# A two-layer encoder trunk on one core: the first two weight units on a second DMA queue, the first tokens turned into two banks, a unit ahead of the parameters

## The reference

```python
def _hybrid_layer(x, cos, sin, ...):
    h = _rms_norm(x, norm_mix)
    z = jnp.einsum('bsd,de->bse', h, w_in)
    za, bq, bk, bv, cq, clat, ciq, cik, ciw, zd, zg = _split(z, IN_SIZES)
    ya = _gmlp_mixer(jax.nn.gelu(za), ...)
    yb = _swa_sink_mixer(bq, bk, bv, ..., cos, sin)
    yc = _dsa_mixer(cq, clat, ciq, cik, ciw, ..., cos, sin)
    yd = _pool_mixer(zd, d_w_group, d_scale)
    gates = jax.nn.sigmoid(zg).reshape(Bsz, S, N_BRANCH, D_MODEL)
    merged = gates[:, :, 0] * (ya @ a_w_out) + ... + gates[:, :, 3] * (yd @ d_w_out)
    x = x + merged @ w_o
    h2 = _rms_norm(x, norm_ffn)
    gate, up = jnp.split(h2 @ w_gate_up, 2, axis=-1)
    return x + (jax.nn.silu(gate) * up) @ w_down
```

## Time and profile before

| | us |
|---|---|
| median of 3 runs (lowest, highest) | 814.96 (814.76, 815.02) |
| the profiled run's own time | 815.25 |
| its span | 813.5 |
| PE busy | 805.1 (99%) |
| PE weight loads busy | 658.0 (81%) |
| DVE busy | 559.7 (69%) |
| ACT busy | 406.1 (50%) |
| POOL busy | 56.6 (7%) |

### The profile page before, as it was taken

One profiled execution on the slowest core, in us unless ns is written; L12 is line 12 of the kernel. 1 busy time (PEld: TensorE's weight loads), 2 busy tenths in 40 slices (PEclk: granted clock), 3 DMA queues, 4 the chain that ended last, 5 costly groups with the idle time before them and its releaser, 6 DMA issues.

```text
span 813.5 us, 10282 instructions
## 1 busy us (share of the span) xinstructions
PE 805.1 (99%) x3872; PEld 658.0 (81%) x3872; DVE 559.7 (69%) x854; ACT 406.1 (50%) x568; POOL 56.6 (7%) x103
## 2 busy tenths in 40 slices
PE   8999999999999999999999999999999999999998
PEld 6788777778888888888888887787788888888886
DVE  7799789877576554566568887898675754565443
ACT  5966655454274434444366644755543643444431
POOL 5850000000000000000005100000000000000000
PEclk9999999999999999999999999999999999999999
DMA  8654536545466555666663625474446555666541
GB/s 301 215 162 136 183 120 208 206 140 183 130 221 206 178 185 161 207 202 192 164 230 116 232 79 182 133 254 156 155 156 207 179 183 166 210 193 198 165 155 52
DMA packets 98976, 144.38 MB, mean 177 GB/s; under 512 B 11112, under 2 KB 62064, under 8 KB 98928
## 3 DMA queue, kind: packets, MB, share of 16 engines
q1 hardware_dynamic: 98928, 143.73, 54.6%
HBM read 142.54 MB, written 1.05 MB: 177 GB/s over the span
## 4 chain that ended last, share of the span: by engine, by line
PE 94%; DMA 2%; DVE 1%; ACT 1%; issue 1%; SPq 1%; ACTq 0%; DVEq 0%
PE big L1537 19%; PE big L1541 19%; PE big L1540 19%; PE mix L1541 10%; PE mix L1537 10%; PE mix L1540 10%; DMA w_raw<-in_w_in 1%; PE mix L1913 1%; PE mix L1581 1%; PE mix L1672 1%; DMA w_raw<-in_w_gate_up 1%; PE mix L1605 1%; PE mix L1593 1%; PE mix L1625 1%; PE mix L1658 1%
## 5 line engine op out<-in xcount | busy, mean ns | idle before, releaser
L738 ACT ACTIVATE w_hi<-w_raw 128x2048 fp32r<-128x2048 f32 (+2 forms) x140 | 255.0, 1827 | 155.4 <-DMA w_raw<-in_w_gate_up 89.6
L1049 DVE TENSOR_TENSOR w_lo<-w_raw,w_hi 128x2048 fp32r<-128x2048 f32 (+3 forms) x142 | 304.6, 2160 | 29.2 <-ACT w_hi L738 27.9
L1537 PE MATMUL big<-w_hi,act_hi 128*128 128x512 f32 (+2 forms) x476 | 185.7, 390 | 2.1 <-DVE w_lo L1049 2.1
L1541 PE MATMUL big<-w_hi,act_lo 128*128 128x512 f32 (+2 forms) x476 | 181.6, 381 | 0.0
L1540 PE MATMUL big<-w_lo,act_hi 128*128 128x512 f32 (+2 forms) x476 | 181.5, 381 | 0.0
L1537 PE MATMUL mix<-w_hi,act_hi 128*128 128x512 f32 x352 | 137.4, 390 | 0.0
L1541 PE MATMUL mix<-w_hi,act_lo 128*128 128x512 f32 x352 | 137.1, 390 | 0.0
L1540 PE MATMUL mix<-w_lo,act_hi 128*128 128x512 f32 x352 | 137.0, 389 | 0.0
L1537 PEld LDWEIGHTS big<-w_hi,act_hi 128*128 128x128 f32 x476 | 89.5, 188 | 22.6 <-DVE w_lo L1049 3.7
L1323 DVE TENSOR_TENSOR y_h_lo<-mix,y_h_hi 128x256 fp32r<-128x256 f32 x44 | 16.6, 420 | 127.7 <-ACT y_h_hi L968 127.7
L1541 PEld LDWEIGHTS big<-w_hi,act_lo 128*128 128x128 f32 x476 | 89.4, 188 | 17.2
(11 more groups left out here) (210 smaller groups left out, 718.6 us busy)
## 6 DMA issues: line engine op xcount, KB each, us to landing
w_raw<-in_w_in SPq DMA_DIRECT2D x44, 1024.0 KB, 5.1
w_raw<-in_w_gate_up SPq DMA_DIRECT2D x88, 512.0 KB, 4.8
w_raw<-in_w_down SPq DMA_DIRECT2D x22, 1024.0 KB, 4.9
w_raw<-in_w_o SPq DMA_DIRECT2D x8, 1024.0 KB, 4.9
w_raw<-in_b_w_out SPq DMA_DIRECT2D x4, 1024.0 KB, 6.3
w_raw<-in_w_in SPq DMA_DIRECT2D x4, 512.0 KB, 4.1
w_raw<-in_a_w_out SPq DMA_DIRECT2D x4, 512.0 KB, 3.5
w_raw<-in_d_w_out SPq DMA_DIRECT2D x4, 512.0 KB, 3.4
```

What stands on the lines that cost most here:

```text
L738: nc.scalar.activation(high(u)[:, a:b], arrived(u)[:, a:b], ACT.Copy).then_inc(hi_ready, 1)
L1049: nc.vector.tensor_tensor(low(u)[:, a:b], arrived(u)[:, a:b], high(u)[:, a:b].bitcast(F32), ALU.subtract).then_inc(lo_ready, 1)
L1537: ins = nc.tensor.matmul(dst[:, 0:w], xh, wh, start=first and n == 0, stop=False)
L1541: ins = nc.tensor.matmul(dst[:, 0:w], xl, wh, start=False, stop=end)
```

## The change

- The loads of units 0 and 1, four halves, are issued by ACT at the head of its program (`load_first`). On SP the tokens, the gain and the positions follow each other, then units 2, 3 and 4.
- Of the first four turned pieces, the last two go to another PSUM bank (`turned_at`). ACT starts once two are turned (`first_turned`). A copy of one element stands ahead, and the scaling of block 1 ahead of the copy of unit 0's second half; DVE and PE are ordered to match. The first projection's second half is taken in portions, both blocks after each.
- Unit 5 (the sixth) is issued ahead of the parameters. Seven parameters follow it; eight others follow unit 7, with a semaphore of their own, on which PE waits at slot 9 and DVE at slot 11.
- ACT squares block 0's tokens ahead of slot 0 and block 1's in slot 0, DVE takes the mean in slot 0, POOL's first power stands ahead of the last steps of the angles. The tables move to slot 2, behind that slot's steps and copies, and the change back to the exponential's table to slot 6.
- In layer 0 DVE ropes the indexer's heads at slots 3 and 4 instead of 2 and 3. At slot 4 the latent's norm now stands ahead of the rope, and the wait for the parameters with it, in both layers.

```diff
-N_PARAMS = 15
+N_PARAMS = 7
+N_LATE_PARAMS = 8
...
+        def turned_at(l, stage, tb, h, j):
+
+            if (l, stage, tb, h) == (0, "hT", 0, 0) and j >= 2:
+                return big[:, main_bank("proj", PROJ[0][0], 1), (j - 2) * P:(j - 1) * P]
+            return mix[:, mix_bank(stage, tb, h), j * P:(j + 1) * P]
...
-                if l == 0 and u < HALVED:
-                    for half, k in ((0, slice(0, 2)), (1, slice(2, 4))):
-                        sp.dma_start(dst[:, k, 0:b], w_in[l, rows, a:a + b].rearrange("(k p) n -> p k n", p=P)[:, k]
-                                     ).then_inc(first_in[u] if half == 0 else landed[s].sem, 16)
-                        if (u, half) == (0, 0):
-                            load_tokens(1, 0)
-                        elif (u, half) == (0, 1):
-                            for tb in range(TB):
-                                load_tokens(tb, 1)
-                            load_positions()
-                elif kind == "in":
+                if kind == "in":
...
-                    (g_ffn[:], norm_ffn[l].rearrange("(k p) -> p k", p=P)),
                     (g_lat[:], c_latent_gain[l].partition_broadcast(P)),
                     (g_head[:, 0], b_q_gain[l].partition_broadcast(P)),
                     (g_head[:, 1], b_k_gain[l].partition_broadcast(P)),
                     (g_head[:, 2], c_q_gain[l].partition_broadcast(P)),
                     (g_head[:, 3], c_k_gain[l].partition_broadcast(P)),
-                    (w_sp[:], a_w_spatial[l].rearrange("g i j -> i g j")),
...
+                assert len(params) == N_PARAMS
+                for dst, src in params:
+                    sp.dma_start(dst, src, allow_slow_non_contiguous=True).then_inc(params_in.sem, 16)
+
+            def load_late_params(l):
+                params = (
+                    (w_sp[:], a_w_spatial[l].rearrange("g i j -> i g j")),
...
+                    (g_ffn[:], norm_ffn[l].rearrange("(k p) -> p k", p=P)),
                 )
-                assert len(params) == N_PARAMS
+                assert len(params) == N_LATE_PARAMS
                 for dst, src in params:
-
-                    sp.dma_start(dst, src, allow_slow_non_contiguous=True).then_inc(params_in.sem, 16)
+                    sp.dma_start(dst, src, allow_slow_non_contiguous=True).then_inc(late_params_in.sem, 16)
...
             load_gain(0)
+            load_tokens(1, 0)
+            for tb in range(TB):
+                load_tokens(tb, 1)
+            load_positions()
             for l in range(DEPTH):
-                load_unit(l, 0)
-                load_unit(l, 1)
+
                 if l > 0:
+                    load_unit(l, 0)
+                    load_unit(l, 1)
                     load_params(l)
+                    load_late_params(l)
                 for u in range(2, NU):
                     load_unit(l, u)
-                    if (l, u) == (0, RING - 1):
+                    if (l, u) == (0, RING):
                         load_params(0)
+                    if (l, u) == (0, RING + 2):
+                        load_late_params(0)
...
                 at = flat[1]
+            power(0, "mix")
             for k, turn in enumerate(TURNS):
...
                 for name in NORMS:
-                    power(l, name)
                     if (l, name) == (0, "mix"):
                         averages_of_pools()
+                    else:
+                        power(l, name)
...
-                nc.scalar.activation(act_spare[:], minus_half[:, 0:1], ACT.Exp).then_inc(alone_act, 1)
+
+            def load_first(u):
+                _, a, b, h = UNITS[u]
+                rows = slice(h * PIECES * P, (h + 1) * PIECES * P)
+                for half, k in ((0, slice(0, 2)), (1, slice(2, 4))):
+                    act.dma_start(w_raw[:, u, k, 0:b], w_in[0, rows, a:a + b].rearrange("(k p) n -> p k n", p=P)[:, k]
+                                  ).then_inc(first_in[u] if half == 0 else landed[u].sem, 16)
...
-                bank = mix_bank("hT", tb, h)
-                act.wait_ge(*mix_is_full(0, "hT", tb, h))
                 for j in range(4):
                     k = 4 * h + j
-                    e = nc.scalar.activation(act_hi[:, k, tok(tb)], mix[:, bank, j * P:(j + 1) * P], ACT.Copy,
+                    if (tb, h, j) == (0, 0, 0):
+                        act.wait_ge(first_turned, 1)
+                    elif j == (2 if (tb, h) == (0, 0) else 0):
+                        act.wait_ge(*mix_is_full(0, "hT", tb, h))
+                    e = nc.scalar.activation(act_hi[:, k, tok(tb)], turned_at(0, "hT", tb, h, j), ACT.Copy,
                                              scale=g_mix[:, k:k + 1])
...
+                    for u in range(HALVED):
+                        load_first(u)
+
+                    act.wait_ge(warm_in, 1)
+                    nc.scalar.activation(act_spare[:], rope_t[:, 0, 0:1], ACT.Copy).then_inc(alone_act, 1)
                     act.wait_ge(gain_placed, 1)
                     first_gained(0, 0)
+                    first_gained(1, 0)
                     split(0, 0, 1)
-                    first_gained(1, 0)
                     first_gained(0, 1)
                     first_gained(1, 1)
                     split(0, 1, 1)
+                    x_squares(0, "mix", 0)
                 for s in range(SLOTS):
-                    if s in STEPS_FIRST:
+                    if s in STEPS_FIRST or (l, s) == (0, 2):
                         steps(l, s)
                     if s == WO + 4:
                         high_gained(l, "h2T", 1)
                     for ahead in splits_in(l, s):
                         split(*ahead)
-                    if (l, s) == (0, 1):
-                        for tb in range(TB):
-                            x_squares(0, "mix", tb)
+                    if (l, s) == (0, 0):
+                        x_squares(0, "mix", 1)
+                    if (l, s) == (0, 2):
                         tables()
-                    if s not in STEPS_FIRST:
+                    if s not in STEPS_FIRST and (l, s) != (0, 2):
                         steps(l, s)
+                    if (l, s) == (0, 6):
+
+                        act.wait_ge(alone_act, 1)
+                        nc.scalar.activation(act_spare[:], minus_half[:, 0:1], ACT.Exp).then_inc(alone_act, 1)
...
                 if s == 1:
                     scales(l, "mix", 0)
-                for tb in range(TB):
-                    if s == 2 + tb:
-                        if l == 0:
-                            dve.wait_ge(const_sin, 4)
-                        dve.wait_ge(*main_is_drained(l, "proj", "idx", tb))
-                        rope(l, "I", heads_a, roped_a, tb, 5, [(0, 4, 1, 0), (4, 5, 2, 4)], tb == 1)
                 if s == 3:
                     mean_of_sums(l, "lat", P)
+                if s == 4:
                     dve.wait_ge(*params_in.nth(l, params_in.per_layer))
-                if s == 4:
                     r = norm_factor(l, "lat")
                     for tb in range(TB):
                         ins = nc.vector.scalar_tensor_tensor(out=lat[:, tb, :], in0=lat[:, tb, :], scalar=r[:, tb:tb + 1],
                                                              in1=g_lat[:], op0=ALU.mult, op1=ALU.mult)
                     ins.then_inc(lat_normed.sem, 1)
+                for tb in range(TB):
+
+                    if s == 2 + tb + (1 if l == 0 else 0):
+                        if l == 0:
+                            dve.wait_ge(const_sin, 4)
+                        dve.wait_ge(*main_is_drained(l, "proj", "idx", tb))
+                        rope(l, "I", heads_a, roped_a, tb, 5, [(0, 4, 1, 0), (4, 5, 2, 4)], tb == 1)
...
+                    dve.wait_ge(*late_params_in.nth(l, late_params_in.per_layer))
...
                     split_high(0)
                     split(0, 0, 0)
                     first_low(0, 0)
+                    first_low(1, 0)
                     split(0, 0, 1)
-                    first_low(1, 0)
                     split_high(1)
                     split(0, 1, 0)
...
-                    if (l, s) == (0, 1):
+                    if (l, s) == (0, 0):
                         mean_of_sums(0, "mix", D_MODEL)
...
-                        ins = nc.tensor.transpose(mix[:, bank, j * P:(j + 1) * P], src[:, tb, k * P:(k + 1) * P],
+                        ins = nc.tensor.transpose(turned_at(l, stage, tb, h, j), src[:, tb, k * P:(k + 1) * P],
                                                   ident[:])
+                        if (l, stage, tb, h, j) == (0, "hT", 0, 0, 1):
+                            ins.then_inc(first_turned, 1)
...
-                    pe.wait_ge(*params_in.nth(l, params_in.per_layer))
+                    pe.wait_ge(*late_params_in.nth(l, late_params_in.per_layer))
...
                     turn(l, "hT", 0, [0])
                     products_of_zeros(2)
-                    first_products(0, 0)
                     turn(l, "hT", 1, [0])
```

(24 more changed lines are left out.)

9 lines of the change are left out of this document (2 added, 7 removed).

## The result

The changed kernel takes 816.09 us (median of 19 runs, 815.28 to 816.67) against 814.59 for the kernel before (19 runs, 813.88 to 815.3) on the same chip: ratio 1.0016, 95% interval 1.0010 to 1.0022. Its profiled execution took 815.43, span 813.7; that of before 815.25, span 813.5.

What follows compares the result with a forecast made beforehand. TensorE is busy 769.40 of 769.71 us from 36.29, so only the first 36.3 us can win. Terms -2.1, +0.2, +1.2, +0.7 sum to 0.0: 815.25 profiled, 815.0 median; 8-in-10 range 812.8 to 816.4.

Steps and rivals of the forecast that it cites:

- the sum: Whole kernel: -2.1 us at the start, +0.2 at unit 3, +1.2 at slot 5, +0.7 at unit 11, together 0.0.
- the slower rival: Positions no sooner, unit 0's subtraction ahead of them, unit 5's in the averages: R 40.2, +1.6 us, 816.6; chance 0.12.
- The chain that was to eat the lead: GpSimd's late latent power delays VectorE's rope to R, cutting TensorE's lead to 0.7 at slot 5 and 0.0 at unit 11.
- the wait at slot 5: Sign of being right: TensorE waits 1 to 3 us before the slot-5 transposes, released by VectorE's rope.
- The start: First 36.3 us: second projection at 19.5 instead of 21.57, a lead of 2.1 us, bounds 1.2 and 2.5.
- The positions: Fewer bytes deep on their queue, so GpSimd may take them 0.8 us sooner than 10.79; bounds 0 and -1.5.
- Unit 5: Issued at 15 instead of 25.99, it lands near 22 to 23, so TensorE's stall of 0.94 us goes.
- The block on GpSimd: Unit 5's subtraction on VectorE falls amid GpSimd's averages and prolongs a select: +2.06 us; latent's power at 35.7 to 36.8.
- R: Time when VectorE has done the latent and block 1's rope at slot 4: 38.2 to 39.3, taken as 38.6.
- The limit at unit 11: VectorE's full row up to unit 11's subtraction caps TensorE's lead at 38.6 - R, 0.0 us.
- The lead kept: Unit 5's subtraction comes after averages and power: R 36.5 to 37.0, lead 1.6 to 2.1, 812.9 to 813.4; chance 0.20.
- The engines' rate as the bound: DMA engines' rate bounds the start, tokens and weights come as before: lead 1.2, R about 39.1, 815.5 us; chance 0.13.

Runs made afterwards that it cites:

- one-queue run: The changed kernel with units 0 and 1 loaded on SyncE again, between the tokens as before: 815.18 us, 0.9997 times the kernel before.
- unit 5 sooner: The kernel before with one line changed, unit 5 issued ahead of the 15 parameters: 814.52 us, 0.9992 times the kernel before.
- power early: The changed kernel with GpSimd doing the mixer norm's power ahead of the third part of the angles' reduction: 816.04 us, 1.0012 times before.
- The fastest kernel: The changed kernel with one queue, rope ahead of latent's norm, last eight selects late and mixer norm's power early: 812.06 us, 0.9964 times before.
- the run that began later (20.59): The changed kernel with units 0 and 1 on SyncE's queue and block 1's rope ahead of the latent's norm in layer 0: 813.47 us, 0.9982 times before.

## Why the prediction was right, point by point

The time lies inside 812.8 to 816.4 and the difference inside what was called no change. But the interval, 1.0010 to 1.0022, does not reach 1: the changed kernel is 1.5 us slower, where the sum gave 0.0, and 816.09 is 1.1 above the forecast of 815.0 and 0.5 below the 816.6 of the slower rival. The chain that was to eat the lead is the one that did. Three of its terms were mis-sized and one step was read wrongly, and that the number held is in part luck, as said below.

Of the signs named beforehand these came: no table load right before the first scaling, the rope that waited for the latent's power, the select of 2.34 over unit 5's subtraction, and the short wait at unit 11. The first scaling (6.30 for 5.7) and the second projection (20.55 for 19.5) missed, the wait at slot 5 was 0.28 for 1 to 3, and the sign set down for the slower rival, a wait for unit 5, was there.

- **The start: 1.0 and not 2.1.** The steps within the engines nearly held: with one queue the second projection was at 19.81 at best, for 19.5 forecast. The main mis-sized term is the arrival of the gain (1.04 of waiting) and of block 1's tokens (0.85); most of it goes with the second queue, and the bound of 1.2 for just this case was still too kind. Over the traces the second projection is at 20.52 to 21.34 with two queues (six traces, mean 20.96, leaving out the one with the positions moved) and 19.81 to 20.59 with one (four, mean 20.18): the second queue costs 0.8 in the mean, as much as the start varies with either, where it was to give speed, and 0.7 of the shortfall against 19.5 is there without it. The engines do move more with it (251 GB/s from 2 to 4 us, where the earlier trace rows has 197), but the bytes that TensorE waits for come later.
- **The positions: 1.0 later and not 0.8 sooner** (11.77 against 10.79 in the earlier trace rows). Outside its bounds of 0 and 1.5 sooner. The rule of the Trainium skill that was weighed ("DMA: Bandwidth & Descriptors", "Issuing engines are not separate DMA queues") says that a second issuer saves issue time only. That it gains nothing here the runs bear out; the one-queue run shows that it can also cost. The same page ("Queues, rings and completion order") says that each DMA engine takes turns between the queues it has work for, a packet from each; the longer landings on both queues agree with that, and no run here looked at packets.
- **Unit 5: the stall did not go.** This step failed. The prediction saw unit 5 issued late and concluded that the queue held it. ScalarE did wait for that DMA before, but VectorE would not have begun the subtraction sooner: it was still in the rope of unit 4's slot. What dated all of it is ScalarE's wait for the mixer norm's power, 3.54 us in the changed kernel. That power came at 23.45, because two steps of the angles took 2.20 and 2.14 over the subtractions of units 2 and 3, where the one ahead of them (16.43) took 0.47. The runs with unit 5 sooner (0.63 left) and with the power early (none left) show it. Cost against the forecast: 1.31.
- **The block on GpSimd: right.** Reckoned 2.06, measured 2.34 less 0.29 is 2.05. That the latent's power ended at 36.68, in the 35.7 to 36.8 given for it, is in part luck: the averages began 0.86 later (24.97 for 24.11), where the sum allowed 0.8 sooner to 0.3 later, and apart from the blocks the averages took 0.5 less than before.
- **R: 39.13 and not 38.6**, in the range of 38.2 to 39.3, near its end because of the positions. That the rope behind the late latent is what costs was confirmed by moving the rope and by moving the selects, 1.6 and 1.5 us by the ratios.
- **The limit at unit 11: right.** The formula 38.6 less R gives -0.5; measured -0.56. The wait at slot 5 was 0.28 and not 1 to 3, since unit 5's had taken the lead before; and since K sets unit 11, TensorE's own delay at unit 5 did not move it: by Q alone it would have been 66.90. So the sum could come out with that step wrong. The lag shrinks to 0.2 by the end of the span, for the kernel before has a stall later which the changed one has not (waits of TensorE, us in total, times, longest):

```profile
PE mix L1581 <- DVE xs L1304: 0.3, 1, 0.3
```

- **The median.** The two profiled executions of the changed kernel (815.43 and 815.35) are among its quickest; its medians are 0.7 to 1.0 above. With its start 0.8 later, as in the power-early run (21.31, and 816.04 for that execution), all that follows is later by as much. That most of its runs start so is argued from this, not shown, and with it 1.3 of the 1.5 us between the medians stand in no trace: the two traces differ by 0.2.
- **The rivals.** The lead kept (0.20) did not happen, for unit 5's subtraction did meet the averages. The engines' rate as the bound (0.13) was nearest in its numbers: lead 1.2 and R 39.1. The slower one (816.6, chance 0.12) had R too late, 40.2 for 39.13, but one of its reasons is what happened at unit 5: the mixer norm's power slipped behind unit 3's subtraction and held ScalarE's first evictions and units 4 and 5 behind them.

Not tried: the two banks or the early table load alone, the late parameters alone, the rope back at slots 2 and 3, and weights on the second queue issued later. The fastest kernel contains all three and has no idle time behind 36.29.

## What to carry to other kernels

Before a lead at the start is counted, follow it through each engine to the first place where two limits cross, and write both as "start of X plus constant"; here two constants, each from one trace, gave unit 11 in eight further kernels. A second queue for big loads made the small ones that gate the first work land later here; try the start with one queue before taking the second for a gain. And a wait whose releaser is late is cured only if the releaser's own order is: here doing one power of 0.7 us ahead of a subtraction of 2.3 us was worth 1.4 us by the medians and 0.8 at unit 11 in the traces, once nothing else held what follows.

## What the runs showed of the hardware

- A GpSimd operation begun a little behind one of VectorE's long subtractions ends only with it (0.29 becomes 2.34; 0.73 becomes 2.66), while one begun 0.06 us ahead of it is not held. Over the 13 traces up to 70 us, all 52 GpSimd operations begun 0.01 to 0.87 behind the start of a subtraction of a 1 MB unit ended 0.14 to 0.59 behind its end (the powers of six columns, 3.3 long, left out), and none of the 32 begun up to 0.29 ahead of it was held. The Trainium skill says the same ("SBUF — State Buffer", "Who interferes with whom": issue order decides who blocks), and the traces agree.
- With one DMA queue the tokens (256 KB) and the positions (1 KB) landed 5.4 and 6.0 us after issue, with two 6.9 and 8.5, while the rate from 2 to 4 us rose from 214 (one-queue run) to 251 GB/s.
- Kernels whose start is the same code began the second projection up to 0.8 us apart (19.81 to 20.59 with one queue), as their first loads landed: VectorE waited 0.73 and 0.21 for halves of units 0 and 1 in the first of these and 1.12 and 0.68 in the second. With VectorE and GpSimd as near to each other as here, this decides whether a block falls: the run that began later (20.59) had the power at 20.93 and unit 5 at 34.33, the one that began at 19.81 had them at 22.91 and 35.15; the rope's place, in which they differ, comes behind both.
